# Three more input tiles turned through DRAM and VectorE, and a new split of the convolution taps

## The reference

```
h = rmsnorm(x, g_mix);  z = h @ w_in            # 1024 -> a (512) | b (512) | v (512)
u = a * sigmoid(b)
u = causal_depthwise_conv(u, conv_w, conv_b)    # 31 taps for each channel
u = silu(layernorm(u, ln_g, ln_b))
q = multiscale_pool(v, pool_w, pool_scale)      # trailing means over 2, 4, 8, 16 positions
x = x + concat(u, q) @ w_out
...
# then a SwiGLU FFN, a gated per-layer input p, and a final norm
```

## Time and profile before

| | us |
|---|---|
| runs, median (lowest to highest) of 3 | 993.95 (993.66 to 994.36) |
| the profiled execution | 992.02 |
| its span in the profile | 990.2 |
| TensorE (PE) busy | 976.5, 99% |
| VectorE (DVE) busy | 712.5, 72% |
| ScalarE (ACT) busy | 464.6, 47% |
| GpSimd (POOL) busy | 390.0, 39% |

### The profile page before, as it was taken

One profiled execution on the slowest core, in us unless ns is written; L12 is line 12 of the kernel. 1 busy time (PEld: TensorE's weight loads), 2 busy tenths in 40 slices (PEclk: granted clock), 3 DMA queues, 4 the chain that ended last, 5 costly groups with the idle time before them and its releaser, 6 DMA issues.

```text
span 990.2 us, 12301 instructions
## 1 busy us (share of the span) xinstructions
PE 976.5 (99%) x4415; PEld 808.9 (82%) x4415; DVE 712.5 (72%) x984; ACT 464.6 (47%) x714; POOL 390.0 (39%) x295
## 2 busy tenths in 40 slices
PE   9999999999999999999999999999999999999996
PEld 7888888878888888888888888888888888888885
DVE  6999899998798355355454454553677888887897
ACT  7735358304464333333333333333444665676865
POOL 3466889711255544444444354451000000012555
PEclk9999999999999999999999999999999999999999
DMA  7731565538725134233333332413998788657432
GB/s 258 142 104 54 99 125 204 170 125 193 202 65 160 54 117 142 60 107 117 97 107 92 121 107 71 141 64 107 358 373 314 238 298 273 195 162 197 152 107 106
DMA packets 175663, 152.94 MB, mean 154 GB/s; under 512 B 73274, under 2 KB 131154, under 8 KB 175602
## 3 DMA queue, kind: packets, MB, share of 16 engines
q1 hardware_dynamic: 174400, 151.76, 49.7%
q10 hardware_dynamic: 1202, 0.40, 0.2%
HBM read 112.02 MB, written 40.11 MB: 154 GB/s over the span
## 4 chain that ended last, share of the span: by engine, by line
PE 76%; DVE 1%; issue 1%; POOL 0%; ACT 0%; POOLq 0%; DVEq 0%; ACTq 0%
PE ps L1743 25%; PE ps L1745 25%; PE ps L1744 25%; PE ps L1794 1%; DVE ftmp L2631 0%; DVE resid L2634 0%; PE ps L1880 0%; POOL rs L841 0%; DVE ring_lo L2103 0%; ACT ftmp L1551 0%; DVE resid L2291 0%; DVE resid L2641 0%; ACT junk L1573 0%; DVE gtmp L2402 0%; DVE ftmp L2624 0%
## 5 line engine op out<-in xcount | busy, mean ns | idle before, releaser
L838 POOL TENSOR_SCALAR ss<-ss 128x1 f32<-128x1 f32 x38 | 16.5, 434 | 322.5 <-ACT junk L1120 287.1
L2202 DVE SCALAR_TENSOR_TENSOR ps<-resid,convw,ps 128x512 f32<-128x512 f32 x184 | 123.4, 748 | 0.0
L1743 PE MATMUL ps<-ring_hi,ring_lo 128*128 128x512 f32 x308 | 119.9, 389 | 0.1
L1744 PE MATMUL ps<-ring_lo,ring_hi 128*128 128x512 f32 x308 | 119.8, 389 | 0.0
L1745 PE MATMUL ps<-ring_hi 128*128 128x512 f32 x308 | 119.8, 389 | 0.0
L1743 PE MATMUL ps<-act_hi,bs_lo 128*128 128x512 f32 x240 | 93.5, 389 | 0.0
L1745 PE MATMUL ps<-act_hi,bs_hi 128*128 128x512 f32 x240 | 93.4, 389 | 0.0
L1744 PE MATMUL ps<-act_lo,bs_hi 128*128 128x512 f32 x240 | 93.4, 389 | 0.0
L2397 DVE TENSOR_TENSOR gtmp<-ps,gtmp 128x512 f32<-128x512 f32 x22 | 15.2, 691 | 95.6 <-PE ps L1745 95.6
L1106 ACT ACTIVATE ring_hi<-raw 128x512 fp32r<-128x512 f32 x89 | 51.9, 625 | 60.4 <-PE ps L1745 60.4
L844 POOL TENSOR_TENSOR wc_lo<-raw_b,wc_hi 128x1024 fp32r<-128x1024 f32 x22 | 55.6, 2526 | 48.9 <-ACT wc_hi L1106 47.8
(11 more groups left out here) (288 smaller groups left out, 2672.4 us busy)
## 6 DMA issues: line engine op xcount, KB each, us to landing
raw<-in_w_gate_up SPq DMA_DIRECT2D x44, 512.0 KB, 5.3
raw<-in_scratch SPq DMA_DIRECT2D x52, 256.0 KB, 3.5
raw<-in_w_down SPq DMA_DIRECT2D x52, 256.0 KB, 4.1
in_scratch<-in_s SPq DMA_DIRECT2D x44, 256.0 KB, 3.4
in_scratch<-gtmp SPq DMA_DIRECT2D x33, 256.0 KB, 2.3
keep<-in_w_down SPq DMA_DIRECT2D x32, 256.0 KB, 4.3
keep<-in_scratch SPq DMA_DIRECT2D x25, 256.0 KB, 3.5
resid<-in_x SPq DMA_DIRECT2D x8, 512.0 KB, 7.0
```

The lines of the kernel that those rows point to most:

```text
L838: pool.tensor_scalar(ss[:, n:n + 1], ss[:, n:n + 1], 1.0 / D, EPS, ALU.mult, ALU.add)\
L1743: pe.matmul(dst, w_lo_, m_hi, start=start, stop=False, skip_group_check=onto)
L1744: pe.matmul(dst, w_hi_, m_lo, start=False, stop=False, skip_group_check=onto)
L2202: dve.scalar_tensor_tensor(out=conv_c if k == last_odd else acc, in0=u_all[:, c, k + h * BANK:k + (h + 1) * BANK], scalar=convw[:, c * 32 ...
```

## The change

Tiles 4, 5 and 6 are no longer turned by TensorE. VectorE normalises them in place; SP stores each to a new DRAM scratch (`store_xa`) and loads it back with 32x32 blocks in their turned places (`load_xa`); VectorE transposes the blocks into PSUM banks 6 and 7 (`x_turn`), from where ScalarE and VectorE make the high and low parts. These pieces stand between the taps of unit 0. Tile 7 is still turned by TensorE and comes before the three (`x_place`).

The low half of weight stripe b0 moves from VectorE to GpSimd, behind `unit_begun(0)`. `OWN` changes from (2, 8, 8, 8, 4, 4, 4, 2) to (2, 8, 10, 10, 6, 4, 4, 0). Units 6 and 7 begin with plain products of VectorE; unit 6's own taps are added at its end by GpSimd (`late_sum`). On GpSimd the sum of unit 4's taps moves ahead of `gate_u(6)` and of v stripes 0 and 1, and `unit_begun(KC)` moves behind v stripe 2. `first_taps(4)` moves ahead of `evac_ab(6)`. In unit 5 the pieces `mix_low_0` and `normed_second` move to earlier taps and `mix_low_2` comes in from unit 6. The core of the diff:

```diff
+        X_DVE = (4, 5, 6)
+        def x_place(t):
+            return t if t < 4 else 4 if t == 7 else t + 1
-        OWN = (2, 8, 8, 8, 4, 4, 4, 2)
+        OWN = (2, 8, 10, 10, 6, 4, 4, 0)
+        LATE = 2 * KC - 2
-            return (0 if t == 7 else 6 - 2 * (t % 2), 4 * (t % 2), 2 if t % 2 == 0 else 0 if t == 1 else 4)[norm]
+            return ((6, 4, 6, 4, 6, 6, 6, 0)[t], 4 * (t % 2), 2 if t % 2 == 0 else 0 if t == 1 else 4)[norm]
...
+            def store_xa(t):
+                sp.wait_ge(xn_ok, t + 1)
+                sp.dma_start(xa_dram[t - 4], x_tile(t, 0)).then_inc(x_in[t], DMA)
+            def load_xa(t):
+                sp.wait_ge(x_in[t], 2 * DMA)
+                for a in range(P // SQ):
+                    src = xa_dram[t - 4].rearrange("(b j) (k a i) -> a j k b i", j=SQ, a=P // SQ, i=SQ)[a]
+                    sp.dma_start(x_tile(t, 0)[a * SQ:(a + 1) * SQ, :].rearrange("j (k b i) -> j k b i", k=KD, i=SQ), src)\
+                      .then_inc(x_in[t], DMA)
+            store_xa(4)
+            store_xa(5)
             sp.wait_ge(w_lo, S_B)
             load_cols(w_in_v, 256, C + 256)
+            load_xa(4)
+            store_xa(6)
+            load_xa(5)
+            load_xa(6)
...
-            sp.wait_ge(taps_done, ops_before(2 * KC - 1) + 2)
+            sp.wait_ge(taps_sum, 2 * KC - 1)
             load_gain(g_ffn[0])
...
             unit_begun(0)
+            pool.wait_ge(w_lo, S_B)
+            split_cols(0, S_B + 1, bs_hi, bs_lo)
...
             unit_begun(3)
+            sum_taps(KC)
             gate_u(6)
...
             gate_u(7)
-            sum_taps(KC)
             split_row(raw_b, 1, bs_hi[:, 3, :], bs_lo[:, 3, :], S_PLE + 2)
-            unit_begun(KC)
             for s in range(2, 4):
                 split_cols(V_STRIPE[s], S_V + s + 1, at=s)
+                if s == 2:
+                    unit_begun(KC)
...
-                if s == 2:
-                    unit_begun(6)
...
+            def late_sum(j):
+                h, c = j // KC, UNIT_C[j]
+                conv_c = conv_o[:, c, h * BANK:(h + 1) * BANK]
+                pool.tensor_tensor(gain[:, 0:BANK], gain[:, 0:BANK], gain[:, BANK:2 * BANK], ALU.add).then_inc(taps_more, 1)
+                pool.wait_ge(taps_more, sums[0] + 1)
+                pool.wait_ge(taps_done, ops_before(j + 1))
+                pool.tensor_tensor(conv_c, conv_c, gain[:, 0:BANK], ALU.add).then_inc(taps_sum, 1)
+            late_sum(LATE)
...
-            turned_hi(4, 0)
-            turned_hi(5, 0)
             square_x(6)
             square_x(7)
             evac_ab(0)
+            first_taps(0)
             split_cols(0, 2 * DMA, bs_hi)
-            first_taps(0)
+            turned_hi(7, 0)
             split_cols(1, 2 * DMA, bs_hi)
-            turned_hi(6, 0)
-            turned_hi(7, 0)
             evac_ab(1)
+            turned_hi(4, 0)
             for m in range(2, 4):
                 split_cols(m, 2 * DMA, bs_hi)
+            turned_hi(5, 0)
             first_taps(1)
+            turned_hi(6, 0)
...
+            first_taps(4)
             evac_ab(6)
...
-            first_taps(4)
             evac_ab(7)
...
-            turn(4, 0)
-            turn(5, 0)
...
                 if n == 2:
+                    pe.wait_ge(act_lo_ok, 2 * x_place(7) + 2)
+                if n == KC:
                     pe.wait_ge(act_lo_ok, 2 * TT)
                 ab_part(n, 0)
                 if n == 1:
-                    turn(6, 0)
                     turn(7, 0)
...
             pe.wait_ge(taps_done, TAPS_ALL)
+            pe.wait_ge(taps_sum, 2 * KC - 1)
             conv_turn(4)
...
+            def x_turn(t):
+                dve.wait_ge(x_in[t], DMA * (2 + P // SQ))
+                dve.wait_ge(act_lo_ok, 2 * x_place(t))
+                dve.transpose(ps[:, 6:8, :].rearrange("p b n -> p (b n)"), x_tile(t, 0)).then_inc(ln_turned, 1)
...
+                    elif plain:
+                        bias = convb[:, c:c + 1] if k == 0 else 0.0
+                        dve.tensor_scalar(acc, u_all[:, c, k + h * BANK:k + (h + 1) * BANK],
+                                          convw[:, c * 32 + k:c * 32 + k + 1], bias, ALU.mult, ALU.add).then_inc(taps_done, 1)
+                        continue
...
+            def last_low():
+                turned_lo(7, 0)
+                dve.wait_ge(w_lo, S_B + 1)
+                b_stripe_low(1)
+            def low_and_turn(t):
+                turned_lo(t, 0)
+                x_turn(t + 1)
-            convolve(0, {1: last_tiles_low})
+            convolve(0, {3: last_low, 4: lambda: x_turn(4), 7: lambda: low_and_turn(4), 10: lambda: low_and_turn(5),
+                         17: lambda: turned_lo(6, 0)})
...
-            convolve(5, {14: normed_first, 22: mix_low_0, 23: normed_second})
-            convolve(6, {1: mix_low_2, 6: lambda: q_low(0), 10: lambda: q_low(1),
+            convolve(5, {14: normed_first, 19: mix_low_0, 20: normed_second, 25: mix_low_2})
+            convolve(6, {6: lambda: q_low(0), 10: lambda: q_low(1),
```

More of the change, by code:

```diff
@@ L76, in hybrid_block @@
     xg_dram = nc.dram_tensor("xg_scratch", (TT, 2, P, BANK), F32, kind="Internal").ap()
+    xa_dram = nc.dram_tensor("xa_scratch", (3, P, D), F32, kind="Internal").ap()
     conv_dram = nc.dram_tensor("conv_scratch", (HT_LN * C, P), F32, kind="Internal").ap()
@@ L174, in turns, with x_trips @@
         def turns(n):
-            by_dve = sum(TT <= k < TT + MIX_TILES or 0 <= k - 2 * TT and k - 2 * TT in DVE_TURNS for k in range(n))
+            by_dve = sum(k in X_DVE or TT <= k < TT + MIX_TILES or 0 <= k - 2 * TT and k - 2 * TT in DVE_TURNS for k in range(n))
             return 2 * (n - by_dve)
         DVE_TURNS = (0, 1, 2, 4, 6)
+        X_DVE = (4, 5, 6)
+        def x_trips(t):
+            return 1 + P // SQ if t in X_DVE else 0
+        def x_place(t):
+            return t if t < 4 else 4 if t == 7 else t + 1
         def dve_turns(t):
@@ L349, in hybrid_block, with first_place @@
         UNIT_C = (0, 1, 2, 3, 2, 3, 0, 1)
-        OWN = (2, 8, 8, 8, 4, 4, 4, 2)
+        OWN = (2, 8, 10, 10, 6, 4, 4, 0)
         def own_place(n):
             return (gain[:, :], scr[:, 2, :], wide[:, 0, HEADPAD:], scr[:, 0, :], scr[:, 1, :])[n]
+        def first_place(j):
+            return own_place(1 if j == 2 * KC - 1 else 0)
         def pairs_before(j):
@@ L1124, in turned_hi @@
                 for j in range(2):
-                    act.wait_ge(turned, 2 * n + j + 1)
+                    if n in X_DVE:
+                        act.wait_ge(ln_turned, X_DVE.index(n) + 1)
+                    else:
+                        act.wait_ge(turned, turns(n) + j + 1)
                     copy(act_hi[:, 4 * j:4 * j + 4, t * P:(t + 1) * P],
@@ L1155, in first_taps @@
                 for k in (*range(2, OWN[j]), 0, 1):
-                    if j and k == 0:
+                    if k == 0 and 0 < j < 2 * KC - 1:
                         act.wait_ge(taps_done, ops_before(j - 1) + 2)
-                    dst = own_place(k // 2)
+                    dst = own_place(k // 2) if k >= 2 else first_place(j)
                     ins = act.activation(dst[:, (k % 2) * BANK:(k % 2 + 1) * BANK],
@@ L1255, in ln_silu @@
                 if n < KC:
-                    act.wait_ge(ln_turned, HT_LN + n + 1)
+                    act.wait_ge(ln_turned, len(X_DVE) + HT_LN + n + 1)
                 else:
@@ L1777, in turn @@
                         pe.wait_ge(xn_ok, n + 1)
-                    if norm == 0 and t >= 2:
+                    if norm == 0 and 2 <= t < 4:
                         pe.wait_ge(act_lo_ok, 2 * n + j - 3)
@@ L2105, in turned_lo @@
             def turned_lo(t, norm, halves=range(2)):
-                n = t if norm == 0 else TT + t
+                n = x_place(t) if norm == 0 else TT + t
                 for j in halves:
@@ L2125, in normed @@
                         dve.wait_ge(xn_turned, n - TT - 1)
-                    else:
+                    elif n not in X_DVE:
                         dve.wait_ge(turned, turns(n - 1))
@@ L2130, in normed @@
                         dve.wait_ge(gain_ok, 2)
-                    ins = dve.scalar_tensor_tensor(out=xn_place(n)[:, c], in0=x_tile(t, norm)[:, c], scalar=rs[:, n:n + 1],
+                    ins = dve.scalar_tensor_tensor(out=(x_tile(t, norm) if n in X_DVE else xn_place(n))[:, c], in0=x_tile(t, norm)[:, c], scalar=rs[:, n:n + 1],
                                                    in1=pair(2)[:, c] if n < 5 else gain[:, c],
@@ L2190, in convolve @@
                 conv_c = conv_o[:, c, h * BANK:(h + 1) * BANK]
-                if OWN[j] > 2:
+                plain = j == LATE or OWN[j] == 0
+                if plain:
+                    dve.wait_ge(u_ok, j + 1)
+                elif OWN[j] > 2:
                     dve.wait_ge(taps_sum, j)
@@ L2204, in convolve @@
                                              scalar=convw[:, c * 32 + k:c * 32 + k + 1],
```

(8 more changed lines are left out.)

10 lines of the change are left out of this document (1 added, 9 removed).

## The result

The changed kernel takes 995.31 us (median of 20 runs, 993.34 to 996.46); the kernel before, run beside it, 993.6 (20 runs, 989.46 to 995.69). The ratio on record is 1.0024, with a 95% interval of 1.0016 to 1.0033: 2.4 us slower. (The two medians alone differ by 1.7.) The profiled execution took 995.70 us, its span is 993.9.

What follows compares the result with a forecast made beforehand. TensorE, busy 99% of 990.2 us, was taken to bound the kernel. Terms -2.7 + 5.3 + 1.4 + 2.4 - 2.6 = +3.8 on 992.0 gave 995.8; the median's 1.9 offset made it 997.8, range 992.0 to 999.8.

Steps and rivals of the forecast that it cites:

- second rival: At unit 4, VectorE's pair enters when GpSimd's running instruction ends, waiting at most 2.4 us; 994.7 us, chance 0.28.
- Transposes, -2.7: Tiles 4 to 6 lose 24 TensorE transposes, so its eight a/b pieces end at 103.3, 2.7 us earlier.
- VectorE, units 0 to 2: Inserted pieces and 2.0 us of trip waits make unit 1 begin at 63.05 and unit 2 at 81.4.
- First V stripe, +5.3: TensorE asks at 103.3 and waits 5.3 us for GpSimd's first low half, done at 108.6.
- Unit 4, 5.9 us of blocking: VectorE arrives at 113.45; its first pair waits 5.9 us until GpSimd's whole train ends at 119.3.
- Evacuations, +1.4: TensorE loses about 1.4 us to evacuations of the V and e stages behind the later `normed_first`.
- second q group, +2.4: TensorE arrives at 171.1 and waits another 2.4 us for VectorE's first q low, ending at 173.55.
- End of the convolution, -2.6: TensorE no longer waits for VectorE's last add and the adds behind it at the convolution turn: 2.6 us won.
- The sum: All terms from transposes to the convolution's end together: +3.8 us, giving 995.8 against the profiled execution's 992.0.
- From 995.8 to 997.8: Added because the runs' median, 993.95, lay 1.9 us above the profiled execution, giving the predicted 997.8.

Runs made afterwards that it cites:

- experiment 2: Changed kernel with 17 small identity products in TensorE's queue ahead of its wait for the first V stripe; 992.48 us, ratio 0.9995.
- trips alone: Also called experiment 4: changed kernel without the part on taps (old `OWN`, no plain products or `late_sum`), keeping the trips through DRAM; 994.02 us, ratio 1.0004.
- experiment 6: Kernel before, with GpSimd waiting for unit 7's first two taps ahead of the third of its four low halves; 989.67 us, ratio 0.9966.
- Experiment 7: Kernel before with only the part on taps, no DRAM trips, and the mix lows and second normalised part back near their old taps; 989.73 us, ratio 0.9984.
- Experiment 5: Kernel before with one edit: unit 7 begins with VectorE's plain products and ScalarE makes no first taps for it; 989.32 us, ratio 0.9967.
- experiment 11: Changed kernel without the part on taps, but units 5 and 7 begin with plain products and q lows stand earlier; 996.27 us, ratio 1.0053.
- experiment 8: Changed kernel with unit 4's sum behind the V stripes again, two unit 3 taps back on VectorE, GpSimd's pause inside the third stripe; 991.99 us, ratio 0.9989.
- experiment 9: The kernel of experiment 8, with VectorE's first q low after tap 4 of unit 6 instead of tap 6; 991.55 us, ratio 0.9984.
- experiment 1: Changed kernel with GpSimd's and ScalarE's old order around the first V stripe, unit 4's sum behind the stripes again; 991.38 us, ratio 0.9982.
- experiment 10: Changed kernel without the part on taps, except that unit 7 begins with plain products; 990.00 us, ratio 0.9986.

## Why the prediction was right, and where it was not

The forecast held in its sign and in what makes the loss: slower, by a wait of TensorE at the first V stripe that outweighs what is won. The time came out 2.5 us under the 997.8 named, inside the whole range, but below the forecast's own 996 to 999.5 and inside the second rival's 993 to 996. Forecast and rival share the wait at the stripe; they part at unit 4, and there the rival was right. By its steps, in the profiled executions:

- **Transposes, -2.7.** TensorE ends piece 7 at 103.67; forecast 103.3, before 106.01: -2.3.
- **VectorE, units 0 to 2.** Unit 0 began at 32.80, not 31.45, but the trips made VectorE wait 0.5 us, not 2.0. By luck the two errors cancel: units 1 and 2 began at 63.04 and 81.38 (forecast 63.05 and 81.4). (The 39.9 for the latest landing does not follow from the 8.7 of the earlier trace rows, which gives 41.6; it did not matter.) The transposes into PSUM took 1.25 to 1.26, as assumed.
- **First V stripe, +5.3.** The wait was 4.43, in the place named and released by the instruction named. What this step lacked is the slow clock behind it, 2.41 us by experiment 2, so its term should have been 6.84. The profiled execution of the kernel before has a 2.1 us wait with a clock of 1.00 behind it, and I took the price of a wait for its length.
- **Unit 4, 5.9 us of blocking.** This step failed. The pair took 4.26, so 2.8 of blocking: the two taps took 1.46 and 2.89, each entering at the end of one GpSimd instruction (113.96 and 116.76) while GpSimd's train went on. I had sided with unit 7's 7.70 us row against the Trainium skill, "SBUF — State Buffer", section "Who interferes with whom", by which the later one blocks until the first finishes. Here the trace agrees with the page. At unit 3 the first tap went in at once, not at the train's end as forecast; the second tap took 2.90 of the pair's 3.58 us and did meet that end, so GpSimd still went on at 99.80 (forecast 100.05). Unit 7's row stays as it was (its first tap, 7.04 us, passed two ends of GpSimd instructions and entered at the third, the train's last): trips alone shows it again (7.83 us for the pair), and experiment 6 shows that GpSimd's standing still ends it. What sets whether a train lets a tap in is open; it was not tried.
- **Evacuations, +1.4; second q group, +2.4.** TensorE arrives there at 171.99, 4.92 later than 167.07. Piece 7, wait and clock explain 4.5 of it (-2.34 + 4.43 + 2.41), which leaves 0.4 for the evacuations. The wait was 0.88. It did not come from unit 4's block: VectorE stood still for 3.00 us in unit 5 for ScalarE, which hid any lateness up to there. Experiment 7 shows, in the kernel without the trips, that a wait of the same length belongs to the moved pieces.
- **End of the convolution, -2.6.** Right: TensorE comes to the turn at 215.52 (forecast 216.3) and waits neither there nor for the adds. The late sum ended at 200.7 (forecast 199). Experiment 5 adds that unit 7's plain products alone bring all of this gain.
- **The sum.** +3.8 was forecast and the spans differ by 3.7, but not by these terms alone: at the first product behind the turn (217.18, before 214.40) the changed kernel is 2.8 behind, and the rest came later, 0.6 of it as one wait that no step of the change names. The runs say 2.4. That the sum agrees is in part luck: the wait and the clock behind it came to 6.84 where 5.3 was forecast, and the two terms after them to 1.3 where 3.8 was.
- **From 995.8 to 997.8.** This term failed. I added the 1.9 by which the median of three lay above the profiled execution, as if that were a cost that both kernels pay. The kernel before scatters over 6 us, and its profiled execution is one with a high clock (0.998; last section); the changed kernel's, 995.70, lies 0.4 above its own median. The sum against the profile would have been the better number.

Of the rivals, the second had the right way of entry at unit 4 (2.4 at most; 2.8 measured), and its 994.7 lies nearer to the 995.31 than the forecast's 997.8; it too left out the slow clock.

## What to carry to other kernels

Price a new TensorE wait by its length and by the slow products behind it; if the wait can't be removed, some idle products in front of it are worth trying. Before an engine is given more work, follow the waits by which others follow it: here a few us on VectorE came back through GpSimd's pauses as waits of TensorE elsewhere. And take a change of many edits apart: one of these edits, unit 7's first two products, alone is 0.33% faster than the kernel before, while all of them together are 0.24% slower (each against the kernel before of its own set).

## What the runs showed of the hardware that was not expected

**The clock falls at short waits, and not by their length alone.** Granted clock at a wait of TensorE, in one execution each: it fell to 0.50 within the waits of 4.43 us (changed kernel) and 4.07 us (experiment 11), and 0.6 to 1.1 us after the end of waits of 2.31 us (experiment 8), 2.27 us (experiment 4, from 213.3), 2.02 us (experiment 9) and 1.87 us (experiment 1, from 152.7). It stayed at 1.00 behind 1.68 us (experiment 10), 1.67 us (experiment 4, at 151.76) and the 2.10 us of the kernel before, which is longer than two of those that made it fall. The Trainium skill, "TensorE: Matmul & The Clock Gate", section "Part 1: The HAM clock gate", says that an idle array's clock goes to 1.2 GHz; the level agrees with the trace (0.50, and 0.43 us for a product instead of 0.23).

**One and the same kernel keeps its clock in some executions and not in others.** Of the 116 executions of the kernel before that ran beside the experiments, 73 had a mean granted clock of 0.997 or 0.998 and a median time of 991.8 us; 43 had 0.996 or less, and 994.1 us. The profiled one (992.02, 0.998) is of the first kind. Of trips alone, four of twelve executions had 0.997 or 0.998 and took 990.65 to 992.45 us; eight had 0.996 or less and took 993.93 to 994.89. Its trace is of the second kind (994.23, 0.996) and has the fall at the convolution turn. No trace of the kernel before with the lower clock was kept, so where its clock falls is not shown; the wait at its turn is the likely place, since without that wait (experiments 5 and 6) all 22 executions had 0.997 or 0.998. One profile of a kernel with such a wait can therefore show a price that many of its executions do not pay, or leave out one that they do.

**GpSimd loses time to a tap that it lets in.** When the first tap of unit 4 entered, the GpSimd row that starts there (113.90) took 2.86 us instead of 2.40; the two instructions that start at the second tap's entry (116.72) took 5.21 us instead of 4.77. In both places some 0.45 us, so the meeting costs both engines.
